# A hybrid decoder block: keys and queries multiplied with both token parts in one 512-column product

## The reference, cut to what matters

```python
u = rms_norm(h, mix_norm_g)
proj = u @ w_in
q, k, v, z, xbc, dt_raw, qm, gate_logits = jnp.split(proj, split_points, axis=-1)
...
s_own = einsum('bhqd,bhjd->bhqj', q_c * d_h ** -0.5, k_own) + bias_tab[:, t5_bucket(dist_own)]
s_own = jnp.where(dist_own >= 0, s_own, -jnp.inf)
p = jax.nn.softmax(s_all, axis=-1)
o = ... + jnp.einsum('bhqj,bhjd->bhqd', p_own, v_own)
```

## Time and profile before

| what | value |
|---|---|
| median of 3 runs | 684.38 us (683.76 to 684.55) |
| the profiled execution's own time | 683.92 us |
| its span, first to last instruction | 682.1 us |
| TensorE busy | 673.5 us, 99% of the span |
| VectorE busy | 493.5 us, 72% |
| ScalarE busy | 371.5 us, 54% |
| bytes moved by DMA | 130.92 MB, 192 GB/s |

### The profile page before, as it was taken

How to read it: one execution, slowest core, us unless ns; L and a number is a source line. 1 busy time by engine, 2 the same in 40 slices (tenths; PEclk the granted TensorE clock), 3 DMA queues, 4 the chain that set the end, 5 groups by cost and what they waited for, 6 DMA issues and landing times.

```text
span 682.1 us, 11417 instructions
## 1 busy us (share of the span) xinstructions
PE 673.5 (99%) x4505; PEld 616.4 (90%) x4505; DVE 493.5 (72%) x617; ACT 371.5 (54%) x462; POOL 10.4 (2%) x21
## 2 busy tenths in 40 slices
PE   8999999999999999999999999999999999999996
PEld 6999999999999989999888888888899999999995
DVE  6886979696866766777754655556688777777796
ACT  7568767767455544555533333443555555555552
POOL 0000000000100000000000000000100000000001
PEclk9999999999999999999999999999999999999999
DMA  9775868569185446545566655565445555555521
GB/s 297 240 256 181 247 198 263 164 217 326 62 270 171 145 163 232 180 140 171 178 211 218 214 194 182 195 231 173 166 140 191 188 185 190 180 189 183 193 87 62
DMA packets 99599, 130.92 MB, mean 192 GB/s; under 512 B 5615, under 2 KB 73708, under 8 KB 98924
## 3 DMA queue, kind: packets, MB, share of 16 engines
q1 hardware_dynamic: 98020, 125.27, 55.8%
q10 hardware_dynamic: 1544, 5.16, 2.3%
HBM read 129.31 MB, written 2.68 MB: 193 GB/s over the span
## 4 chain that ended last, share of the span: by engine, by line
PE 97%; DVE 1%; DMA 1%; ACT 0%; POOL 0%; issue 0%; POOLq 0%; SPq 0%; DVEq 0%; ACTq 0%
PE ps L364 31%; PE ps L365 30%; PE ps L366 30%; PE ps L678 1%; DMA x_nat<-x 1%; PE ps L679 1%; PE ps L419 1%; PE ps L663 1%; PE ps L698 1%; PE ps L715 1%; PE ps L706 0%; DVE h_nat L1750 0%; PE ps L697 0%; PE ps L717 0%; PE ps L771 0%; PE ps L666 0%
## 5 line engine op out<-in xcount | busy, mean ns | idle before, releaser
L336 DVE TENSOR_TENSOR w_lo<-w_raw,w_hi 128x2048 fp32r<-128x2048 f32 x107 | 244.6, 2287 | 88.0 <-ACT w_hi L332 88.0
L332 ACT ACTIVATE w_hi<-w_raw 128x2048 fp32r<-128x2048 f32 x107 | 204.3, 1911 | 99.1 <-PE ps L366 93.9
L364 PE MATMUL ps<-tok_hi,w_hi 128*128 128x256 f32 x864 | 246.6, 285 | 0.4 <-DVE tok_lo L1310 0.4
L365 PE MATMUL ps<-tok_lo,w_hi 128*128 128x256 f32 x864 | 244.4, 283 | 0.0
L366 PE MATMUL ps<-tok_hi,w_lo 128*128 128x256 f32 x864 | 244.4, 283 | 0.0
L364 PEld LDWEIGHTS ps<-tok_hi,w_hi 128*128 128x128 f32 x864 | 165.7, 192 | 2.0 <-issue 1.5
L365 PEld LDWEIGHTS ps<-tok_lo,w_hi 128*128 128x128 f32 x864 | 165.7, 192 | 0.4
L366 PEld LDWEIGHTS ps<-tok_hi,w_lo 128*128 128x128 f32 x864 | 165.7, 192 | 0.0
L364 PE MATMUL ps<-w_hi,tok_hi 128*128 128x512 f32 x128 | 50.2, 392 | 0.0
L365 PE MATMUL ps<-w_lo,tok_hi 128*128 128x512 f32 x128 | 49.9, 390 | 0.0
L366 PE MATMUL ps<-w_hi,tok_lo 128*128 128x512 f32 x128 | 49.8, 389 | 0.0
(11 more groups left out here) (269 smaller groups left out, 1002.2 us busy)
## 6 DMA issues: line engine op xcount, KB each, us to landing
w_raw<-w_in SPq DMA_DIRECT2D x94, 512.0 KB, 4.8
w_raw<-w_ffn_up SPq DMA_DIRECT2D x44, 512.0 KB, 4.4
w_raw<-w_ffn_down SPq DMA_DIRECT2D x22, 512.0 KB, 4.1
w_raw<-w_mem_kv SPq DMA_DIRECT2D x16, 512.0 KB, 4.4
w_raw<-w_br_ssm SPq DMA_DIRECT2D x16, 512.0 KB, 4.9
acs_b<-acs_d ACTq DMA_DIRECT2D x4, 1024.0 KB, 6.3
w_raw<-w_br_attn SPq DMA_DIRECT2D x8, 512.0 KB, 4.8
w_raw<-w_br_mem SPq DMA_DIRECT2D x8, 512.0 KB, 4.6
```

The source lines that it names most:

```text
L332: act.activation(w_hi[:, s, :], w_raw[:, s, :], ACT.Copy).then_inc(hi_ready[s], 1)
L336: dve.tensor_tensor(w_lo[:, s, :], w_raw[:, s, :], w_hi[:, s, :].bitcast(F32), ALU.subtract).then_inc(lo_ready[s], 1)
L364: pe.matmul(o, a[0], b[0], start=start, stop=False, **kw)
L365: pe.matmul(o, a[0], b[1], start=False, stop=False, **kw)
```

## The change: what it does

Four things change in the stretch of keys and queries; the rest of the kernel is as it was.

1. The two token parts lie side by side in one tile `tok`, `[8 steps, 2 parts, 256 tokens]`. For key and query chunks a new helper `gemm_both` issues two products for each step and column tile: `w_hi` by both parts (512 columns, one whole bank) and `w_lo` by the high part (256 columns, onto the first half of that bank). The second half of the bank holds `w_hi` by `tok_lo`, and each column tile has a bank of its own: 0 and 1 for keys, 3 and 4 for the queries of round 0, 6 and 7 for the later ones.
2. ScalarE copies the second halves of the two banks to `k_t` or `q_t` (semaphore `low_part`), and VectorE adds the first halves to them. `bank_free` comes from VectorE's addition.
3. In a round, keys and queries now follow each other; `attend` and `turn_probs` come behind the queries. `attend(1)` and `attend(2)` write into bank 0, behind a wait for VectorE's addition of that round's keys.
4. `m_factor_kept` and `m_factor_in` become one semaphore.

```diff
-    tok_hi = place("tok_hi", 72, [KT, T], F32R)
-    tok_lo = place("tok_lo", 80, [KT, T], F32R)
+    tok = place("tok", 72, [KT, 2, T], F32R)
+    tok_hi, tok_lo = tok[:, :, 0, :], tok[:, :, 1, :]
...
+    def gemm_both(pe, s, banks, both, other=None):
+        for j in range(2):
+            if other is not None and j:
+                pe.wait_ge(*other)
+            for k in range(KT):
+                w = slice(k * CW + j * P, k * CW + (j + 1) * P)
+                pe.matmul(ps[:, banks[j], :], w_hi[:, s, w], both[:, k], start=k == 0, stop=False)
+                mm = pe.matmul(ps[:, banks[j], 0:T], w_lo[:, s, w], both[:, k, 0, :], start=False, stop=k == KT - 1)
+        mm.then_inc(gemm_done[s], 1)
...
     def attend_bank(n):
-        return (7, 7, 2, 6)[n - 1]
+        return (0, 0, 2, 6)[n - 1]
...
+            def keys(i):
+                pe.wait_ge(lo_ready[0], RB + i + 2)
+                pe.wait_ge(bank_free[0], RB + i + 1)
...
+                if i == 1:
+                    pe.wait_ge(y_step, GT * GROUPS)
+                if i > 2:
+                    pe.wait_ge(oa_lo_s, i - 2)
+                gemm_both(pe, 0, K_BANKS, tok)
...
             for i in range(1, 4):
-                gemm_cols(pe, RB + i, 0, tok_hi, tok_lo)
+                keys(i)
+                queries(i)
                 if i > 1:
-                    pe.wait_ge(oa_lo_s, i - 2)
-                    pe.wait_ge(group_var, 1)
+                    pe.wait_ge(bank_free[0], RB + 2 + i)
                     attend(i - 1)
                 turn_probs(i)
-                gemm_cols(pe, RB + i, 1, tok_hi, tok_lo)
                 gemm_wide(pe, RB + i, i % 2, tok_hi, tok_lo)
                 if i == 1:
+                    pe.wait_ge(bank_free[1], RB + 3)
                     group_sums()
                 scores(i)
...
             def heads(i, first=False):
                 r = RB + i
+                act.wait_ge(gemm_done[0], r + 1)
+                act.activation(k_t[:], part_pair(K_BANKS, 1), ACT.Copy).then_inc(low_part, 1)
                 split_hi(act, r + 1, 0)
+                act.wait_ge(gemm_done[1], r + 1)
+                act.activation(q_t[:], part_pair(q_banks(i), 1), ACT.Copy, scale=DH ** -0.5).then_inc(low_part, 1)
                 if i > 1:
                     attended_hi(i - 1)
...
-                act.wait_ge(gemm_done[1], r + 1)
-                act.activation(q_t[:], halves(1), ACT.Copy, scale=DH ** -0.5).then_inc(bank_free[1], 1)
                 split_hi(act, r + 1, 1)
...
-                dve.wait_ge(gemm_done[0], r + 1)
-                dve.tensor_copy(k_t[:], halves(0)).then_inc(bank_free[0], 1)
+                dve.wait_ge(low_part, 2 * i + 1)
+                dve.tensor_tensor(k_t[:], part_pair(K_BANKS, 0), k_t[:], ALU.add).then_inc(bank_free[0], 1)
                 split_lo(dve, r + 1, 0)
+                dve.wait_ge(low_part, 2 * i + 2)
+                dve.scalar_tensor_tensor(q_t[:], part_pair(q_banks(i), 0), DH ** -0.5, q_t[:], ALU.mult,
+                                         ALU.add).then_inc(bank_free[1], 1)
```

More of the change, by code:

```diff
@@ L65 @@
 HK = KT // 2
+K_BANKS = (0, 1)
 V_BANKS, G1_BANKS, OUT_BANKS, H_BANKS = (2, 5), (0, 7), ((2, 3), (6, 7)), (4, 5, 0, 3)
@@ L269, in build @@
         sem, ("group_mm", "group_var", "group_pow", "group_kept", "rstd_g_in"))
+    low_part = sem("low_part")
     s_mm, s_biased, s_max, s_neg, p_exp, p_rec, p_norm, p_turned, pt_ready, o_mm, oa_hi_s, oa_lo_s = map(
@@ L274, in build @@
     norm_step, os_hi_s, os_lo_s = map(sem, ("norm_step", "os_hi_s", "os_lo_s"))
-    m_in, m_sumsq, m_var, m_rstd, m_scaled, mx_in, m_factor_kept, m_factor_in, m_hi, m_lo = map(
-        sem, ("m_in", "m_sumsq", "m_var", "m_rstd", "m_scaled", "mx_in", "m_factor_kept", "m_factor_in", "m_hi", "m_lo"))
+    m_in, m_sumsq, m_var, m_rstd, m_scaled, mx_in, m_factor_moved, m_hi, m_lo = map(
+        sem, ("m_in", "m_sumsq", "m_var", "m_rstd", "m_scaled", "mx_in", "m_factor_moved", "m_hi", "m_lo"))
     ms_mm, ms_max, ms_neg, mp_exp, mp_rec, mp_norm, mp_turned, mo_mm, om_hi_s, om_lo_s = map(
@@ L432, in halfcols, with q_banks, part_pair @@
         return slice(n % 2 * (D // 2), (n % 2 + 1) * (D // 2))
+    def q_banks(i):
+        return (6, 7) if i else (3, 4)
+    def part_pair(banks, n):
+        return ps[:, banks[0]:banks[1] + 1, n * T:(n + 1) * T]
     def attend_bank(n):
-        return (7, 7, 2, 6)[n - 1]
+        return (0, 0, 2, 6)[n - 1]
     def halves(b):
@@ L719, in attend, with queries @@
                 mm.then_inc(o_mm, 1)
-            gemm_cols(pe, RB, 0, tok_hi, tok_lo)
-            gemm_cols(pe, RB, 1, tok_hi, tok_lo)
+            def keys(i):
+                pe.wait_ge(lo_ready[0], RB + i + 2)
+                pe.wait_ge(bank_free[0], RB + i + 1)
+                if i == 0:
+                    pe.wait_ge(bank_free[1], RB + 1)
+                if i == 1:
[3 more added lines that the diff above has]
+                gemm_both(pe, 0, K_BANKS, tok)
+            def queries(i):
+                pe.wait_ge(lo_ready[1], RB + i + 2)
+                pe.wait_ge(bank_free[1], RB + i + 1)
+                if i == 0:
+                    pe.wait_ge(xdt_ready, NT * GROUPS)
+                gemm_both(pe, 1, q_banks(i), tok, (group_var, 1) if i == 2 else None)
+            keys(0)
+            queries(0)
             scan(GROUPS)
@@ L1110, in _ @@
             act.wait_ge(m_rstd, NT)
-            act.dma_start(m_factor_d.rearrange("(p t) -> p t", p=P), stat[:, 2:2 + NT]).then_inc(m_factor_kept, 16)
+            act.dma_start(m_factor_d.rearrange("(p t) -> p t", p=P), stat[:, 2:2 + NT]).then_inc(m_factor_moved, 16)
             def mem_high(j):
@@ L1117, in _ @@
             squares(GROUPS)
-            act.wait_ge(m_factor_kept, 16)
-            act.dma_start(m_factor[:], on_all(m_factor_d, T)).then_inc(m_factor_in, 16)
+            act.wait_ge(m_factor_moved, 16)
+            act.dma_start(m_factor[:], on_all(m_factor_d, T)).then_inc(m_factor_moved, 16)
             for i in range(1, 4):
@@ L1517, in heads @@
                 if i == 1:
-                    dve.wait_ge(m_factor_in, 16)
+                    dve.wait_ge(m_factor_moved, 32)
                     dve.wait_ge(mx_in, 16)
```

## The result

The changed kernel takes 685.45 us (median of 18 runs) against 684.32 us of the kernel before (18 runs) beside it: ratio 1.0016, 95% interval 1.0009 to 1.0024. The forecast was 684.8, no measurable change, own range 684.5 to 686.2. The loss is real, but about a sixth of a percent. The profiled execution took 685.59 us.

The account below looks back on a forecast made before the run. TensorE, waiting for nothing in this stretch, was taken as the bound. Merged products (−1.47 us) plus attend(1)'s wait (+1.88) gave +0.41 us, hence 684.8 us; this case's own range was 684.5 to 686.2, the overall range 683.0 to 686.0.

Parts of the forecast that it names:

- The wait of attend(1): Round 2, behind the queries: TensorE waits 1.88 us for VectorE's key addition to free bank 0, all lost.
- The bounds, 1.77 and 2.15: Wait at attend(1): 1.77 us if VectorE starts earlier, 2.15 if its PSUM addition costs as much as the bias addition.
- No wait at i = 3: Attend(2) in round 3: bank 0 is free 0.17 us before TensorE arrives; put at zero, at most 0.3 us.
- The merged product: Key and query chunks: a step costs 0.3473 in place of 0.3588 us, saving 1.47 us over eight chunks.
- The stated bounds, 0 to 1.60: Merged-product saving: 1.60 us by the best wide pitch, 0 if alternating widths makes the wide product as dear as two narrow.
- pairs dearer than 0.35 us: Sign of being wrong: key and query pairs of 512 and 256 columns taking longer than the expected 0.347 us.
- The formula of the Trainium skill: N / 2.4 + 2.5 ns per streamed product; one product fewer worth 2.5 ns, 0.32 us in all; the forecast preferred the trace.
- The rival of a small saving: Key and query chunks: mixed widths cost more, saving only 0.3 us, wait 1.6, time 685.7 us; chance 0.10.
- The wait does not come: Rival at attend(1): the low copy or softmax chain is early enough, the whole saving stays, 682.9 us; chance 0.12.
- Slower, by the clock: Rival behind attend(1)'s wait: granted clock falls to 1.2 GHz, costing 1.3 us more, 686.1 us; chance 0.10.
- What costs nothing: Elsewhere in the stretch: other new waits, later turning of probabilities, weight splits, the single semaphore and extra copies add no time.
- The sum: Whole change: saving of 1.47 us and wait of 1.88 us give +0.41 us, 684.8 us; likeliest case, chance 0.68.

Follow-up runs that it names:

- e1: Changed kernel with VectorE's scaling and ScalarE's rounding of the memory tokens moved one round later; 683.13 us, ratio 0.9992 to the kernel before.
- e13: e1 with only the first two steps of each key chunk grouped as 512, 512, 256, 256 columns; 682.37 us, ratio 0.9978 to the kernel before.
- e9: Changed kernel with ScalarE's four memory rounding copies done twice, to lengthen the wait; 689.24 us, ratio 1.0071 to the kernel before.
- e7: e1 with each column tile's eight 512-column products first, then its eight of 256; 682.82 us, ratio 0.9985 to the kernel before.
- e10: e1 with all sixteen 512-column products of a chunk first, then all sixteen of 256; 682.72 us, ratio 0.9985 to the kernel before.

## Why the prediction was right, and where not

**The wait of attend(1): right.** Forecast 1.88 us, measured 1.86 by the timeline and 1.89 by taking it away. Each link was as worked out: the low copy directly behind the fourth me_hi, 0.60 us (0.58 in its row), VectorE 0.03 us behind it, its addition 0.69. The bounds, 1.77 and 2.15, weren't needed. That it came within 0.03 us has some luck in it: round 2 is the one round at the quick pace. At 0.3533 us a pair TensorE would have come to attend(1) some 0.21 us later (32 pairs, an estimate), for a wait of about 1.65. That the stage before hides nothing, because TensorE is the bound on both sides, is shown by e1: all of the wait came back.

**No wait at i = 3: right,** by 0.37 us in place of 0.17 (VectorE ready at 240.47 + 0.68 + 0.16 = 241.31, TensorE at 241.68), for TensorE came later than forecast.

**The merged product: the term that was mis-sized.** The prediction's step was "A step then costs 0.3473 in place of 0.3588 us", the sum of two paces that were each read from a stream of one width. In the mixed stream a step costs 0.3533 in rounds 0, 1 and 3 and 0.3467 in round 2: 32 × (3 × 0.0055 + 0.0121) = 0.92 us by these paces, 0.94 by the stretch. The stated bounds, 0 to 1.60, held it. Among the prediction's signs of being wrong stood "pairs dearer than 0.35 us", and three rounds of four show them. Had all four rounds been entered as e13 enters them, the saving would have been 1.56 and the sum about +0.3 us, near the forecast; that is an estimate, for no run has e13's order and the wait together. The trace of before could not show which it would be: it has no chunk of weights with both widths.

The formula of the Trainium skill ("TensorE: Matmul & The Clock Gate", Back-to-back issue gap), by which one product fewer is worth 2.5 ns, is not borne out here. The section calls it the gap of an isolated product and sets it apart from a stream in which each product has a weight load of its own, as here; the prediction took it for a stream. Undoing the merge costs 1.05 us over 128 products, 8 ns each, and 12 ns at the quick pace. The narrow pitch, 119.6 ns, lies 10.4 ns above what the formula gives, 109.2, and not "11 to 12" as the prediction has it.

The rival of a small saving, 0.3 us, is false in size: the saving is three times that. Its condition was met in part, as in three rounds two widths in turn cost more than each alone (0.3533 us against 0.3473). Its time, 685.7 us, lies nearer to the 685.45 measured than the forecast's 684.8, since the saving fell between the two and the wait did not shrink.

**The rivals.** "The wait does not come" is false in the changed kernel; e1 shows that it would have been worth 1.89 us, and that the reason given against it (the four copies in ScalarE's queue) was most of the cause. "Slower, by the clock" is false at this wait, with a granted clock of 1.00 behind it. e9 shows that the mechanism exists: at 3.9 us it is there and costs 1.65 us, near the 1.3 that was read from the kernel's start. The change lies on the safe side of it by less than 2.1 us.

**What costs nothing: right.** No other wait of the changed kernel in the stretch stands in its list, and the one elsewhere comes and goes with a transfer.

**The sum.** −0.94 + 1.86 = +0.92 us against the forecast's +0.41; the runs show +1.1 and +0.9. The 0.5 us between them is the saving; gain and loss were both where the forecast put them.

What stays open is why the alternation has two paces and what in the products ahead sets which one. Round 2 differs from the others in that the group sums, eight products of 256 columns, stand just ahead of the scores that precede it; no run here moved them.

## What to carry to other kernels

Before an engine's work is moved behind a new releaser, look at what stands ahead of that releaser in its queue, even work of another branch: four roundings of the memory tokens, which nobody needed yet, cost more than the whole merge saved, and moving them, with the scaling that they wait for, by one round turned 0.13% lost into 0.08% gained (the gain by an interval that just reaches none). A pace that was read from a stream of one shape may not be carried to a mixed stream without a margin; here it cost a third of the saving, and the order of the first four products decided it. A wait on the bound engine costs its own length only while the clock stays full; a wait twice as long cost 1.65 us on top of its length.

## What the runs showed of the hardware that was not expected

- The same alternation of 512 and 256 columns runs at 0.3533 or 0.3467 us a pair. The pace is set at its entry and holds for a chunk or more, through all 64 products of a round: in the slow one the distances of the starts repeat over three pairs, in the quick one over two (e1, e13).
- In a run of one width, the first five to ten products of 512 columns take 224 to 236 ns each, those after 226 or 227 (e7, e10).
- A wait of 3.9 us brought the granted clock to 0.50, and the fall came about a microsecond after the work had resumed; one of 1.86 us left it at 1.00.
- One product of 512 columns in place of two of 256 saves 8 to 12 ns at full clock.
